# Joined: modulation sums closed by one product per group and 32x32 turns on VectorE, and another order of projections and levels in the mixers

## The reference, cut to what matters

```python
def adaln(cond, w, b):
    mod = jax.nn.silu(cond) @ w + b
    return jnp.split(mod, 6, axis=-1)

sh_m, sc_m, g_m, sh_f, sc_f, g_f = (t[:, None, :] for t in adaln(c, ada_w[i], ada_b[i]))
csh_m, csc_m, cg_m, csh_f, csc_f, cg_f = adaln(c_ctx, ada_w[i], ada_b[i])
```

```python
b = jnp.cumsum(g_c, axis=2)
rel = b[:, :, :, None, :] - b[:, :, None, :, :]
decay = jnp.where(causal, jnp.exp(jnp.where(causal, rel, 0.0)), 0.0)
A = jnp.einsum('bhtk,bhsk,bhtsk->bhts', q_c, k_c, decay)
o_intra = jnp.einsum('bhts,bhsv->bhtv', A, v_c)
```

## Time and profile before

| | |
|---|---|
| median of three runs | 2688.91 us (2684.37 to 2692.07) |
| profiled execution | 2690.2 us, its span 2688.4 us |
| TensorE (PE) busy | 2504.8 us, 93% |
| VectorE (DVE) busy | 1499.8 us, 56% |
| ScalarE (ACT) busy | 1058.9 us, 39% |
| GpSimd (POOL) busy | 322.3 us, 12% |

### The profile page before, as it was taken

One profiled execution on the slowest core, in us unless ns is written; L12 is line 12 of the kernel. 1 busy time (PEld: TensorE's weight loads), 2 busy tenths in 40 slices (PEclk: granted clock), 3 DMA queues, 4 the chain that ended last, 5 costly groups with the idle time before them and its releaser, 6 DMA issues.

```text
span 2688.4 us, 36315 instructions
## 1 busy us (share of the span) xinstructions
PE 2504.8 (93%) x14419; PEld 2159.4 (80%) x14419; DVE 1499.8 (56%) x2860; ACT 1058.9 (39%) x1888; POOL 322.3 (12%) x231
## 2 busy tenths in 40 slices
PE   7988889999998999998799999999899998899998
PEld 6877767887888787777598888888877877788887
DVE  4565556757766677777855434343645456533334
ACT  5544434222224555555521121212555555422223
POOL 2212100000003122211100000000332322000001
PEclk9999989999998999999799999999999999899999
DMA  4111023445441111111033333342121212232231
GB/s 115 47 47 48 24 95 114 157 156 167 147 145 48 32 40 39 34 39 41 31 108 117 117 94 122 102 132 73 36 56 44 56 52 60 75 98 87 97 107 54
DMA packets 236578, 218.59 MB, mean 81 GB/s; under 512 B 26164, under 2 KB 205146, under 8 KB 236410
## 3 DMA queue, kind: packets, MB, share of 16 engines
q1 hardware_dynamic: 236410, 216.27, 26.4%
HBM read 214.01 MB, written 2.22 MB: 80 GB/s over the span
## 4 chain that ended last, share of the span: by engine, by line
PE 76%; DVE 11%; ACT 7%; issue 4%; POOL 1%; SPq 0%; DMA 0%; DVEq 0%; POOLq 0%; ACTq 0%
PE ps L368 23%; PE ps L369 22%; PE ps L370 22%; PE ps L657 1%; DVE FR L532 1%; PE ps L1076 1%; ACT whi L393 1%; PE ps L2431 1%; ACT FA L2524 1%; PE ps L2888 1%; DVE hT L2604 1%; ACT FR L527 1%; DVE FA L2644 1%; ACT FA L2957 1%; PE ps L2901 1%
## 5 line engine op out<-in xcount | busy, mean ns | idle before, releaser
L368 PE MATMUL ps<-Uh,whi 128*128 128x512 f32 (+2 forms) x2544 | 902.8, 355 | 19.5 <-ACT FA L2543 5.9
L369 PE MATMUL ps<-Ul,whi 128*128 128x512 f32 (+2 forms) x2544 | 888.8, 349 | 0.0
L370 PE MATMUL ps<-Uh,wlo 128*128 128x512 f32 (+2 forms) x2544 | 887.8, 349 | 0.0
L368 PEld LDWEIGHTS ps<-Uh,whi 128*128 128x128 f32 x2544 | 491.8, 193 | 86.3 <-issue 11.9
L370 PEld LDWEIGHTS ps<-Uh,wlo 128*128 128x128 f32 x2544 | 490.6, 193 | 59.8
L369 PEld LDWEIGHTS ps<-Ul,whi 128*128 128x128 f32 x2544 | 491.7, 193 | 57.4
L393 ACT ACTIVATE whi<-raw 128x1024 fp32r<-128x1024 f32 (+2 forms) x205 | 296.4, 1446 | 543.6 <-PE ps L370 543.4
L404 DVE TENSOR_TENSOR wlo<-raw,whi 128x2048 fp32r<-128x2048 f32 (+2 forms) x121 | 248.5, 2054 | 299.8 <-ACT whi L393 299.6
L368 PE MATMUL ps<-FR,whi 128*128 128x512 f32 (+1 forms) x864 | 302.9, 351 | 7.3 <-DVE wlo L404 4.8
L369 PE MATMUL ps<-FR,whi 128*128 128x512 f32 (+1 forms) x864 | 300.1, 347 | 0.0
L370 PE MATMUL ps<-FR,wlo 128*128 128x512 f32 (+1 forms) x864 | 299.6, 347 | 0.0
(11 more groups left out here) (349 smaller groups left out, 3012.0 us busy)
## 6 DMA issues: line engine op xcount, KB each, us to landing
FA<-in_ada_w_dram SPq DMA_DIRECT2D x192, 256.0 KB, 2.8
raw<-in_ffn_w_gate_up_dram SPq DMA_DIRECT2D x44, 1024.0 KB, 5.1
raw<-in_ffn_w_down_dram SPq DMA_DIRECT2D x24, 768.0 KB, 4.3
raw<-in_w_in_dram SPq DMA_DIRECT2D x29, 512.0 KB, 3.9
raw<-in_da_wqkv_dram SPq DMA_DIRECT2D x24, 512.0 KB, 3.8
raw<-in_na_wqkv_dram SPq DMA_DIRECT2D x24, 512.0 KB, 3.8
raw<-in_w_ffn_gate_dram SPq DMA_DIRECT2D x11, 1024.0 KB, 5.4
raw<-in_w_ffn_up_dram SPq DMA_DIRECT2D x11, 1024.0 KB, 5.4
```

Of the source, the lines that this page charges most:

```text
L368: e.matmul(out, ah, bh, start=start, stop=False)
L369: e.matmul(out, ah, bl, start=False, stop=False)
L370: return e.matmul(out, al, bh, start=False, stop=stop)
```

## The change

Two edits are joined. The first closes a modulation group in another way. On VectorE each condition's accumulator (128 x 512) is turned in blocks of 32 x 32 into the other group's accumulator, and summed along each block to 16 columns; then one matmul with a matrix that is one where two partitions agree modulo 32 sums the rest on TensorE, 32 or 16 columns for both conditions at once. The modulation then reads its sums in four pieces of 32 partitions. The second edit changes the order of `fill` in the mixers: both halves of `gv`, the turn of its result and half of the next head's `fk` come ahead of level 0, `fv` comes ahead of `fq`, `gate` ahead of levels 6 and 7 (in the last head ahead of all levels). And `spare` leaves a bank that was given to `gq` or `gate` out of the round for the next six requests.

```diff
+        self.same_lane = self.causalf
@@ ada_vector
         if k == 0:
             w.wait_ge(*K.was("ada_sum", g - 2))
+            if g:
+                w.wait_ge(*K.at("a_sum", g - 1, ada_conditions(g - 1)[-1]))
@@
+def ada_quadrants_vector(K, e, w, g, c):
+
+    w.wait_ge(*K.was("ada_sum", g - 1))
+    w.wait_ge(*K.at("ada", KC * g + KC - 1, c))
+    if c:
+        w.wait_ge(*K.at("a_sum", g, 0))
+    turned = K.ada_acc[2 * ((g + 1) % 2)]
+    e.transpose(turned, K.ada_acc[2 * (g % 2) + c]).then_inc(*K.ev("t_sum", g, c))
+    w.wait_ge(*K.at("t_sum", g, c))
+    e.tensor_reduce(K.ada_acc[2 * (g % 2)][:, 16 * c:16 * c + 16], turned.rearrange("p (b k) -> p b k", k=32), AX.X,
+                    ALU.add).then_inc(*K.ev("a_sum", g, c))
+
+def same_lane_vector(K, e, w):
+
+    w.wait_ge(*K.at("const_r", 1))
+    w.wait_ge(*K.at("ident"))
+    for b in range(4):
+        i = e.tensor_reduce(K.same_lane[:, 32 * b:32 * b + 32], K.ident[:, :].rearrange("p (a n) -> p n a", a=4), AX.X, ALU.add)
+    i.then_inc(*K.ev("l_sum"))
@@ ada_sum_tensor
-    w.wait_ge(*K.at("ada", KC * g + KC - 1, cs[-1]))
-    for q in range(4):
-        for c in cs:
-            t = e.matmul(o[:, 2 * q + c:2 * q + c + 1], K.ada_acc[2 * (g % 2) + c][:, q * P:(q + 1) * P], K.ones[:, 0:1],
-                         start=True, stop=True)
+    w.wait_ge(*K.at("l_sum"))
+    w.wait_ge(*K.at("a_sum", g, ada_conditions(g)[-1]))
+    e.matmul(o[:, 0:n], K.same_lane[:, :], K.ada_acc[2 * (g % 2)][:, 0:n], start=True, stop=True).then_inc(*K.ev("ada_sum", g))
@@ ada_mod_vector
+    for b in range(4):
+        r = slice(32 * b, 32 * b + 32)
+        i = e.tensor_tensor(K.mod[l][r, q0:q0 + 4, 0:n], sums[r, :, :, b], bias[r, :, :], ALU.add)
+    i.then_inc(*K.ev("mod", g))
@@ mixers_steps
-        fill = [(0, ("split", j, "gv")), (3, ("gv", j, 0)), (0.9, ("level", j, 0)), (3, ("gv", j, 264)), (0.9, ("level", j, 1)),
-                (0.7, ("turn_gv", j, 0))]
+        fill = [(0, ("split", j, "gv")), (3, ("gv", j, 0)), (3, ("gv", j, 264)), (0.7, ("turn_gv", j, 0))]
         if j < 3:
-            fill += [(0, ("split", m, "fk")), (3, ("fk", m, 0)), (0.9, ("level", j, 2)), (3, ("fk", m, 264)), (0.9, ("level", j, 3)),
+            fill += [(0, ("split", m, "fk")), (3, ("fk", m, 0)), (0.9, ("level", j, 0)), (3, ("fk", m, 264)), (0.9, ("level", j, 1)),
+                     (0, ("split", m, "fv")), (3, ("fv", m, 0)), (0.9, ("level", j, 2)), (3, ("fv", m, 264)), (0.9, ("level", j, 3)),
                      (0, ("split", m, "fq")), (5.4, ("fq", m, 0)), (0.9, ("level", j, 4)), (0.6, ("keys", j, 0)),
-                     (0, ("split", m, "fv")), (3, ("fv", m, 0)), (0.9, ("level", j, 5)), (1.9, ("table", m, 0)),
-                     (0.9, ("states", j, 0)), (3, ("fv", m, 264)), (0.9, ("level", j, 6)), (0.9, ("level", j, 7)),
-                     (0, ("split", j, "gate")), (5.4, ("gate", j, 0)), (1.7, ("output", j, 0)),
+                     (1.9, ("table", m, 0)), (0.9, ("level", j, 5)), (0.9, ("states", j, 0)),
+                     (0, ("split", j, "gate")), (5.4, ("gate", j, 0)), (0.9, ("level", j, 6)), (0.9, ("level", j, 7)),
+                     (1.7, ("output", j, 0)),
         else:
-            fill += [(0.9, ("level", j, 2)), (0.9, ("level", j, 3)), (0, ("split", j, "gate")), (5.4, ("gate", j, 0)),
-                     (0.9, ("level", j, 4)), (0.6, ("keys", j, 0)), (0.9, ("level", j, 5)), (0.9, ("states", j, 0)),
+            fill += [(0, ("split", j, "gate")), (5.4, ("gate", j, 0)), (0.9, ("level", j, 0)), (0.9, ("level", j, 1)),
+                     (0.9, ("level", j, 2)), (0.9, ("level", j, 3)), (0.9, ("level", j, 4)), (0.6, ("keys", j, 0)),
+                     (0.9, ("level", j, 5)), (0.9, ("states", j, 0)),
@@ hgrn_tensor
-        b = K.xbank[what, h, n] = spare()
+        b = K.xbank[what, h, n] = spare(6 if what in ("gq", "gate") else 0)
@@ mixers_tensor
-    def spare():
-        ring.append(ring.pop(0))
-        return ring[-1]
+    def spare(skip=0):
+        b = next(b for b in ring if not skips[b])
+        for r in ring:
+            skips[r] = max(0, skips[r] - 1)
+        skips[b] = skip
+        ring.remove(b)
+        ring.append(b)
+        return b
@@ ffn_vector
         elif what == "ada":
+            if s == 0:
+                same_lane_vector(K, e, w)
+            if s % KC == 0 and s > f.a0 and len(ada_conditions(s // KC - 1)) > 1:
+                ada_quadrants_vector(K, e, w, s // KC - 1, 1)
             ada_vector(K, e, w, s)
+            if s % KC == KC - 1:
+                ada_quadrants_vector(K, e, w, s // KC, 0)
+                if s + 1 == f.a1 and len(ada_conditions(s // KC)) > 1:
+                    ada_quadrants_vector(K, e, w, s // KC, 1)
```

More of the change, by code:

```diff
@@ L664, in ada_mod_vector @@
     w.wait_ge(*K.at("ada_sum", g))
+    sums = K.bank(K.ada_bank[g])[:, 0:16 * n].rearrange("p (c q b) -> p q c b", c=n, b=4)
     bias = K.cols[:, 128 + 48 * l + q0:132 + 48 * l + q0].unsqueeze(2).broadcast_to([P, 4, n])
-    e.tensor_tensor(K.mod[l][:, q0:q0 + 4, 0:n], K.bank(K.ada_bank[g])[:, 0:8].rearrange("p (q c) -> p q c", c=2)[:, :, 0:n], bias,
-                    ALU.add).then_inc(*K.ev("mod", g))
+    for b in range(4):
+        r = slice(32 * b, 32 * b + 32)
+        i = e.tensor_tensor(K.mod[l][r, q0:q0 + 4, 0:n], sums[r, :, :, b], bias[r, :, :], ALU.add)
+    i.then_inc(*K.ev("mod", g))
 def prelude_sync(K, e, w):
@@ L1116, in mixers_tensor @@
 def mixers_tensor(K, e, w):
-    ring, held = [4, 5, 6, 7], {}
-    def spare():
-        ring.append(ring.pop(0))
-        return ring[-1]
+    ring, held, skips = [4, 5, 6, 7], {}, [0] * 8
+    def spare(skip=0):
[6 more added lines that the diff above has]
+        return b
     for what, j, x in mixers_steps():
```

3 lines of the change are left out of this document (1 added, 2 removed).

## The result

The changed kernel takes 2662.64 us (median of four runs, 2657.93 to 2669.32), the kernel before, run beside it, 2689.09 us; the ratio is 0.9902, 95% interval 0.9886 to 0.9917. That is 26 us less where 48 were forecast: faster, as predicted, at 2662.6 against a range that ended at 2662. The profiled execution has a span of 2660.7 us, 27.7 less than before.

What follows compares the result with a forecast made beforehand. PE, busy for 93% of the span, was taken as the bound. From 2690.2 us, 25 us (first edit) and 23 us (second) go, giving 2642; the median lies 1.3 us under, so 2641 us, range 2624 to 2662.

Steps and rivals of the forecast that it cites:

- The new sum: TensorE's closing of a modulation group: one matmul of 2 records, taken at 0.24 us, at worst 0.5 us.
- The pair: VectorE's turn and block sum of 128x512 for each accumulator: 1.4 us a pair, between 0.9 and 2.8 us.
- the added wait of PE's sum: PE's modulation sums in the feed-forwards wait for the second condition's block sum; 5 us of the saving come back.
- Group 1: Modulation sum in f0: PE already waits 0.35 us for the accumulation, so 2.5 us more wait.
- Group 6: Modulation sum in f0: 1.81 us of the 2.8 us wait are covered, 1.0 us is not.
- Group 8: Modulation sum in f0, like group 6: 0.9 us of added wait.
- (a): Level 0 of heads 1 and 2: waits for `scaled` go, 8.2 us, plus 3.4 us of clock behind them.
- (b): Turn of the last query block: three waits for gq's bank shrink by 1.35 us each, 4.1 us, plus 1.7 us of clock.
- (c): Ten short waits at later levels in the mixers, 6.4 us: half let go, 3 us.
- (d): Last head: gate ahead of all levels, VectorE bounds the stretch behind it, output some 25 us after gate; 3 us go.
- Rival 3: Mixers: level waits move instead of going, or the clock falls in packed levels; second edit keeps 8 us, 2656 us; chance 0.12.
- clock counted as a gain: Mixers: time at the lowered clock behind removed waits returns, 3.4 us at level 0 and 1.7 us behind gq's bank waits.

Runs made afterwards that it cites:

- e3: The changed kernel with banks handed out in plain turn, without the skip for gq and gate; 2667.57 us, ratio 0.9909 to the kernel before.
- e5: The changed kernel with TensorE's sum of each modulation group one step later, step 3 in place of 2; 2655.37 us, ratio 0.9878 to the kernel before.
- e6: The changed kernel with the bank of gq or gate left out for five requests in place of six; 2661.12 us, ratio 0.9900 to the kernel before.
- e15: The kernel before with fv's first half moved ahead of level 4, so short products follow one another; 2687.33 us, ratio 0.9984 to the kernel before.
- e11: e9 with 16 added, overwritten products of 512 columns in each of heads 0 to 2; 2649.86 us, ratio 0.9848 to the kernel before.
- e9: The changed kernel with sums at step 3, five skips, and levels 0 to 2 ahead of gate in the last head; 2657.01 us, ratio 0.9867.

## Why the prediction was wrong in size

**First edit: near in size, with one term too small.** The new sum is 0.37 - 0.23 = 0.14 us plus 0.1 us for its successor, 0.24 as taken, at 32 columns. The pair is 0.71 + 0.69 = 1.39 us, as taken; the two-input operations of rows 6 were the right neighbours for both halves. By the Trainium skill, "VectorE: DVE Perf Modes", The three transpose paths, the turn alone would have been 1.24 us, an estimate from four times its 311 ns for 128x128 in bf16; it took 0.71. The Trainium skill, "VectorE: DVE Perf Modes", Rules for kernel authors, calls `tensor_reduce` the slowest operation of this engine; the row of 686 ns beside 692 to 746 ns in rows 6 does not bear that out here.

The failed step is the added wait of PE's sum. Forecast were 2.5, 1.0 and 0.9 us more at groups 1, 6 and 8 and 0.6 at the end of f0, 5 us. Measured are 8.0 us more at the sums (8.3, less the 0.35 of before) and 0.5 at the last modulation.

- Group 1: PE had already waited 0.35 us for the accumulation, and the forecast took that off the 2.8 us of the two pairs. A wait that is there leaves no slack. 0.35 + 2.8 is 3.15 us, and 3.23 were measured.
- Group 6: the distance between VectorE's accumulation and PE's sum was read from the trace of before, where PE still had the old sums to do. Each sum is now 1.6 us shorter, and VectorE has no pause there: 1.0 + 1.6 is 2.6, measured 2.65:

```profile
637.10 0.38 PE L681 MATMUL ps<-FA,causalf 128*128 128x32 f32 x2 [2.65 <-DVE FA L661]
```

- Group 8: VectorE itself waits for PE just ahead of it (2.10 us in both traces), so the distance stayed, and the forecast of 0.9 is near the 1.03 measured.
- Groups 9 and 2 (1.08 and 0.32 us) were missed. At group 9 another operation of VectorE (0.6 us) also comes between the two pairs.

The clock, for which nothing was taken, falls behind groups 1 and 6, but f0 as a whole has as much of it as before, 19.5 and 19.3 us.

**Second edit: 23 forecast, 12 at full clock, 7.5 measured.** Most of what is missing is here. The failed step is that waits were taken as gone that passed to another product or bank, and that the clock was counted as a gain.

- (a) The level 0 waits of heads 1 and 2 went nearly as forecast: in head 1 level 0 waits 0.62 us in place of 4.09, and a later one 1.22.
- (b) The wait for the bank of gq went too, but the next one in the round came up: `spare` hands gk the bank of `sums`, whose reader on ScalarE is late by 1.5 us, and a turn waits 0.6. "Which is free at 135.4" was right for one bank; who gets the bank that the old order would have given was not followed to the end. Gain by e3 0.6 us a head in heads 0 to 2, not 1.35, and none in all.
- (c) Of the short level waits half was to go. VectorE's masked copies are still late; the table waits for them now (2.3 us) and the output (1.9 us). Gain none.
- (d) The last head gained 2.6 us of 3: its output comes at 352.93, where it was at 364.17, with 8.6 us of that from the heads ahead. Gate ends 15.3 us into the head, for the forecast 16. But behind it the output takes 27.9 us and not 25, and VectorE is busy for 22.1 of them, so it isn't the bound all the way as the forecast had it; 10.24 us of that stretch are at the low clock. That the size fits is in part luck.

In sum the idle time from 60 to 400 us fell by 10.4 us and not 18.3. And the clock gave nothing back: 5.1 us were counted, and the mean of the old and new orders differs by as much the other way. Rival 3, at 2656 us, held both accounts, waits that move and a clock that falls in packed levels, and came out nearest; it left 8 us of the second edit, which alone measured 7.5, so its chance of 0.12 was too small.

**The sum.** Forecast were 48.7 us ahead of rounding (25.3 and 23.4). Less 3.5 for the first edit's waits (8.5 for 5), 7.9 for idle time in the mixers (10.4 for 18.3), 5.1 of clock counted as a gain and 5.6 of clock lost, 26.6 remain where 26.4 were measured. The last term is a mean over kernels with a wide scatter, and of the first edit alone 3 us more are missing at full clock (19 for 25.3 - 3.5) that no run locates, so the close fit is chance. The range ended at 2662, since it counted rival 3 and the first edit's waits each alone, and no clock worse than before.

## What to carry to other kernels

If an edit makes the busiest engine faster, the waits that remain have to be worked out from where that engine will be, not from where it was: where the other engine has no pause, take the saving off the distance, and where it waits for the busy engine itself, leave the distance as it is. Trying the consumer of the other engine's result one step later is cheap (e5: 7.7 us in f0 for one digit, 3.5 of it idle time), but look where the waits come back. When a bank or buffer is taken out of a round, write down who gets each one afterwards; the wait that was removed here passed in part to the next in the round. And count no gain of the clock from a removed wait when the order of products changes too, and compare kernels by span times granted clock as well as by the median.

## What the runs showed of the hardware

The clock fell to 1.2 GHz for 13.6 us while PE was never idle, behind 6 us with 0.8 us of idle time (e6, three times in one execution), and stayed at 2.4 GHz in e15 behind 10 us with 2.3 us of idle time. The prediction read falls as the price of waits of 4 us; in the mixers the order of the products has a part in them too, 5 to 6 us by the two groups of kernels. The Trainium skill, "TensorE: Matmul & The Clock Gate", Part 4: PE-mode transpose, says of this engine's transpose mode that it does not count as PE-busy in the same way. The stretches that fell are full of products by the identity, which would fit. But e15's stretch has the same ones and kept its clock, and no run here took the turns alone away. With 10.9 us of added work that was overwritten, e11 was no slower than e9: 13.6 us came back by the clock.
